# Pre-summed gates written without adding, and table work spread anew over the mixer, in a transformer layer with product-key experts

## The reference, cut to what matters

```
h = layer_norm(alpha * h + mixer(h))                   # z = h @ w_in; attention; s5 scan; glu; up; out
# experts: 8 heads; keys i and j of 128 each
v_half, i_half = top_k(q @ sub_keys, 16)
top_sc, pos = top_k(all sums of one i and one j, 16)
experts = 128 * i + j ;  gates = softmax(top_sc)
act = gelu(einsum('btd,btrkd->btrk', h, u_table[experts]))
y   = einsum('btrk,btrkd->btd', gates * act, v_table[experts])
out = layer_norm(alpha * h + y + ple)
```

## Time and profile before

| | |
|---|---|
| median of 3 runs | 4163.25 us (4162.76 to 4163.94) |
| the profiled execution | 4163.33 us, span in the trace 4161.5 us |
| busy over the span | PE 90%, DVE 67%, POOL 59%, ACT 27% |
| granted clock, mean | 0.958 |
| POOL L829, scatters | 384, 766.4 us busy, mean 1996 ns |
| DVE L1768, turns in the mixer | 162, 192.0 us busy, 370.2 idle ahead of them |
| DVE L2170, dots | 128, 293.1 us busy, 418.6 idle ahead of them |

### The profile page before, as it was taken

How to read it: one execution, slowest core, us unless ns; L and a number is a source line. 1 busy time by engine, 2 the same in 40 slices (tenths; PEclk the granted TensorE clock), 3 DMA queues, 4 the chain that set the end, 5 groups by cost and what they waited for, 6 DMA issues and landing times. The chain is left out here.

```text
span 4161.5 us, 48848 instructions
## 1 busy us (share of the span) xinstructions
PE 3732.4 (90%) x17969; PEld 3234.3 (78%) x17969; DVE 2785.7 (67%) x3191; ACT 1139.3 (27%) x1377; POOL 2446.1 (59%) x1290
## 2 busy tenths in 40 slices
PE   6999999999979999999999558888844999999998
PEld 5777787777767788799999558888843888888887
DVE  7666666667732557695555145555546999999998
ACT  3222222232211422233323112222211323333332
POOL 6333333334434244465555888777786888887871
PEclk9999999999999999999999779999976999999999
DMA  6888888878878578989999468888878999999995
GB/s 226 289 286 291 292 281 288 287 269 293 283 253 272 204 260 325 406 297 337 312 274 277 91 216 295 293 288 278 295 236 298 382 371 396 373 385 383 379 378 194
DMA packets 452613, 1231.10 MB, mean 296 GB/s; under 512 B 120568, under 2 KB 165640, under 8 KB 370984
## 3 DMA queue, kind: packets, MB, share of 16 engines
q1 hardware_dynamic: 261784, 770.07, 53.4%
q0 software_dynamic: 106496, 302.31, 21.2%
q10 hardware_dynamic: 84240, 157.63, 10.3%
HBM read 1020.65 MB, written 344.45 MB: 328 GB/s over the span
## 5 line engine op out<-in xcount | busy, mean ns | idle before, releaser
L764 POOL TENSOR_TENSOR wlo<-raw,whi 128x1024 fp32r<-128x1024 f32 x296 | 755.4, 2574 | 1078.2 <-ACT whi L1117 526.9
L1310 PE MATMUL bank<-h_hi,whi 128*128 128x384 f32 (+1 forms) x3312 | 1206.1, 364 | 191.1 <-DVE wlo L1637 188.0
L1311 PE MATMUL bank<-h_lo,whi 128*128 128x384 f32 (+1 forms) x3312 | 1191.8, 360 | 0.0
L1312 PE MATMUL bank<-h_hi,wlo 128*128 128x384 f32 (+1 forms) x3312 | 1191.8, 360 | 0.0
L829 POOL DMA_INDIRECT gates_d<-sel_g,place_u x384 | 766.4, 1996 | 303.7 <-issue 295.7
L1310 PEld LDWEIGHTS bank<-h_hi,whi 128*128 128x128 f32 x3312 | 633.9, 191 | 257.5 <-DVE wlo L1637 204.5
L1312 PEld LDWEIGHTS bank<-h_hi,wlo 128*128 128x128 f32 x3312 | 633.2, 191 | 50.2
L1311 PEld LDWEIGHTS bank<-h_lo,whi 128*128 128x128 f32 x3312 | 634.0, 191 | 47.7 <-issue 0.2
L1608 PE MATMUL bank<-whi,ew_hi 128*128 128x512 f32 x1408 | 550.3, 391 | 115.1 <-DVE ew_lo L1637 112.3
L1637 DVE TENSOR_TENSOR wlo<-raw,whi 128x2048 fp32r<-128x2048 f32 x240 | 549.0, 2288 | 144.1 <-ACT whi L1236 89.2
L2170 DVE SCALAR_TENSOR_TENSOR u_row<-u_row,h_tok 128x2048 f32<-128x2048 f32 x128 | 293.1, 2290 | 418.6 <-DMA u_row<-u_rows_d,expert_u 418.5
(11 more groups left out here) (299 smaller groups left out, 4645.3 us busy)
## 6 DMA issues: line engine op xcount, KB each, us to landing
raw<-in_weights SPq DMA_DIRECT2D x388, 1024.0 KB
v_rows_d<-in_weights ACTq DMA_DIRECT2D x96, 1024.0 KB
tin<-in_weights SPq DMA_DIRECT2D x162, 512.0 KB, 6.0
u_rows_d<-tout SPq DMA_DIRECT2D x324, 256.0 KB, 6.7
u_rows_d<-u_tout SPq DMA_DIRECT2D x188, 256.0 KB
v_rows_d<-in_weights SPq DMA_DIRECT2D x32, 1024.0 KB
gates_d<-zeros SPq DMA_DIRECT2D x32, 768.0 KB, 17.2
act_d<-act_o ACTq DMA_DIRECT2D x128, 192.0 KB
```

The lines of the kernel that those rows point to most:

```text
L764: pool.tensor_tensor(wlo[slot][:, part], raw[slot][:, part], whi[slot][:, part].bitcast(F32), ALU.subtract).then_inc(lo_made, 1)
L1310: pe.matmul(bank, whi[slot][:, cols], rhs_hi(c), start=c == 0, stop=False)
L1311: pe.matmul(bank, whi[slot][:, cols], rhs_lo(c), start=False, stop=False)
L1312: last = pe.matmul(bank, wlo[slot][:, cols], rhs_hi(c), start=False, stop=c == DC - 1)
```

## The change

1. A scatter no longer adds. From the second head on it writes a gate from `gate_all`, in which DVE's new `sum_gates(k)` has put, for each token and tile, the sum of the gates of the same cell over all picks up to the end of k's head. 112 picks x 3 tiles are 336 scalar_tensor_tensor operations of 128 x 32 to 128 x 128, with a drain ahead of each three, nine in each unit from 16 on, behind the low part. A scatter of tile 0 waits for the sums of its pick.
2. FIRST_SCATTERS 215 instead of 200. Units 16 to 65 turn a slab (50 instead of 47). Dots come 2.25 per unit from unit 69 on, the last in unit 125.
3. OUT has 9 turns instead of 12, three per group. There are two tout buffers; turns of UP and OUT use them alternately, the heads one.
4. In a mixer head slot(3) stands directly behind slot(2), ahead of the wait for h_filled and of the scan; slot(5) ahead of divide(2) and divide(3).
5. Row copies: six per head at b = 0 to 5, 8 in the GLU, 32 in the queries, 16 in the gates stage, 24 in units 0 to 11 (two each).
6. SP in OUT: behind wide load 12 the wait for all stores, ln_g, ln_b, the wait for h_ready, pw_sb, p_sb, then wide loads 13 to 15.

```diff
 HEAD_STEPS = 7 * HEADS - 3
-UP_STEPS, OUT_STEPS = 16, 12
+UP_STEPS, OUT_STEPS = 16, 9
 STEPS = HEAD_STEPS + UP_STEPS + OUT_STEPS
...
 U_ROWS = 3
-U_LAYS = SB - HEADS - N_GLU // 2 - (N_Q // 2 - 1) - N_GATE // 2
-FIRST_SCATTERS = 200
+HEAD_LAYS = 6
+GLU_LAYS_AT = HEAD_LAYS * HEADS // 4
+Q_LAYS_AT = GLU_LAYS_AT + N_GLU // 2
+GATE_LAYS_AT = Q_LAYS_AT + N_Q // 2
+U_LAYS_AT = GATE_LAYS_AT + N_GATE // 4
+U_LAYS = (SB - U_LAYS_AT) // 2
+FIRST_SCATTERS = 215
...
-    return 67 + 4 * k // 7
+    return TURN_U.stop + 3 + 4 * k // 9
...
     tin = [sb(f"tin{h}", [P, HALF], c_at + 4 * h * kb) for h in range(2)]
-    tout = sb("tout", [P, 4, DC, 32], c_at + 8 * kb)
+    tout = [sb(f"tout{k}", [P, 4, DC, 32], c_at + at * kb) for k, at in enumerate((8, 24))]
     u_tout = [sb(f"u_tout{k}", [P, 4, DC, 32], c_at + 8 * k * kb) for k in range(2)]
...
     expert_f = sb("expert_f", [P, PICKS], c_at + 20.5 * kb)
+    gate_all = sb("gate_all", [P, TD, PICKS], c_at + 21 * kb)
+    same = sb("same", [P, TD, PICKS], c_at + 22.5 * kb)
...
     tin_landed = [sm("tin_landed0"), sm("tin_landed1")]
-    tr_made, tout_stored = sm("tr_made"), sm("tout_stored")
+    tr_made = sm("tr_made")
+    tout_stored = [sm("tout_stored0"), sm("tout_stored1")]
     tab_stored = [sm("tab_stored0"), sm("tab_stored1")]
...
         return sum(len(POOL_TILES[n]) for n in range(first))
+    def turned_in(x):
+        q = x - HEAD_STEPS
+        return (0, x) if q < 0 else (1, q // 2) if q % 2 == 0 else (0, HEAD_STEPS + q // 2)
+    TOUTS = [HEAD_STEPS + (STEPS - HEAD_STEPS) // 2, (STEPS - HEAD_STEPS + 1) // 2]
...
                 if x > 0:
-                    store_rows(tout, step_slab(x - 1), tout_stored)
+                    k = turned_in(x - 1)[0]
+                    store_rows(tout[k], step_slab(x - 1), tout_stored[k])
...
                     load_slab(8 * i + b + 2, b % 2)
-                    if b % 2 == 1:
-                        lay_rows(sp, i, b // 2)
+                    if b < HEAD_LAYS:
+                        lay_rows(sp, (HEAD_LAYS * i + b) // 4, (HEAD_LAYS * i + b) % 4)
                     if b == 1:
...
                 table_step(HEAD_STEPS + UP_STEPS - 2 + i)
+            load_wide(AT_OUT, N_OUT - 4)
+            for k in range(2):
+                sp.wait_ge(tout_stored[k], 64 * TOUTS[k] + 64 * (1 - k))
+            sp.dma_start(ln_g[:, :], row(2)).then_inc(ln1_landed, 16)
+            sp.dma_start(ln_b[:, :], row(3)).then_inc(ln1_landed, 16)
             sp.wait_ge(h_ready, TT)
...
             sp.dma_start(p_sb[:, :, :], p_t).then_inc(ple_landed, 16)
-            for i in range(N_OUT - 4, N_OUT):
+            for i in range(N_OUT - 3, N_OUT):
                 load_wide(AT_OUT, i)
-                if HEAD_STEPS + UP_STEPS - 2 + i <= STEPS:
-                    table_step(HEAD_STEPS + UP_STEPS - 2 + i)
-            sp.wait_ge(tout_stored, 64 * (STEPS + 1))
-            sp.dma_start(ln_g[:, :], row(2)).then_inc(ln1_landed, 16)
-            sp.dma_start(ln_b[:, :], row(3)).then_inc(ln1_landed, 16)
             for i in range(2):
...
                     pool.wait_ge(gate_placed[t], 16 * k)
+                if k >= TOPK and t == 0:
+                    pool.wait_ge(gates_summed, TD * (k - TOPK + 1))
                 pool.indirect_dma_start(out=places_d,
                                         out_offset=bass.IndirectOffsetOnAxis(ap=place_u[:, t, k:k + 1], axis=0),
-                                        in_=sel_g[:, t, k:k + 1], in_offset=None, compute_op=ALU.add
+                                        in_=(sel_g if k < TOPK else gate_all)[:, t, k:k + 1], in_offset=None
                                         ).then_inc(gate_placed[t], 16)
...
             pool.wait_ge(tables_made, 1)
-            pool.wait_ge(tout_stored, 64 * (STEPS + 1))
             for k in range(2):
+                pool.wait_ge(tout_stored[k], 64 * TOUTS[k] + 64 * (1 - k))
                 pool.wait_ge(tab_stored[k], 64 * TURNED[k])
...
                     for c in range(2):
-                        lay_rows(act, HEADS + j, 2 * s + c)
+                        lay_rows(act, GLU_LAYS_AT + j, 2 * s + c)
...
-            def queries(start, end, more=None, lays=True):
+            def queries(start, end, more=None):
                 with act.Fori(start, end) as j:
...
                         next_hi(AT_Q, j, s, blk_done, BLK_Q + o)
-                        if lays:
-                            for c in range(2):
-                                lay_rows(act, HEADS + N_GLU // 2 + j, 2 * s + c)
+                        for c in range(2):
+                            lay_rows(act, Q_LAYS_AT + j, 2 * s + c)
                         act.wait_ge(blk_done, BLK_Q + o + 1)
...
             queries(0, DC // 4, squares)
-            queries(DC // 4, DC // 2 - 1)
-            queries(DC // 2 - 1, DC // 2, None, False)
+            queries(DC // 4, DC // 2)
             act.wait_ge(ms_ready, 1)
...
                 next_hi(AT_GATE, o // 2, o % 2, blk_done, BLK_GATE + o)
-                for c in range(2):
-                    lay_rows(act, HEADS + N_GLU // 2 + N_Q // 2 - 1 + o // 2, 2 * (o % 2) + c)
+                lay_rows(act, GATE_LAYS_AT + o // 4, o % 4)
                 if o % 4 == 0 and o > 0:
...
                     if lays:
-                        lay_rows(act, j + SB - U_LAYS, s)
+                        for c in range(2):
+                            lay_rows(act, 2 * j + U_LAYS_AT + s // 2, 2 * (s % 2) + c)
                     act.wait_ge(blk_done, BLK_U + e + 1)
...
-            def turn_slab(x):
-                dve.wait_ge(tout_stored, 64 * x + 64)
+            def turn_slab(x, k=0, used=None):
+                if k == 0:
+                    dve.wait_ge(tout_stored[0], 64 * (x if used is None else used) + 64)
+                elif used > 0:
+                    dve.wait_ge(tout_stored[1], 64 * used)
                 for h in range(2):
                     dve.wait_ge(tin_landed[h], 16 * x + 16)
-                    dve.transpose(out=tout[:, :, 8 * h:8 * h + 8, :].rearrange("p e c i -> p c e i"),
+                    dve.transpose(out=tout[k][:, :, 8 * h:8 * h + 8, :].rearrange("p e c i -> p c e i"),
                                   in_=tin[h][:, :].rearrange("p (c e j) -> p c e j", c=8, e=4)).then_inc(tr_made, 1)
...
                 slot(2)
+                slot(3)
                 dve.drain()
...
                     tt(h_st[:, :, :, 1 + 2**k:], h_st[:, :, :, 1 + 2**k:], ta, ALU.add)
-                    if k == 2:
-                        slot(3)
                     dve.drain()
...
                 bias_and_max(3)
+                slot(5)
                 divide(2)
                 divide(3)
-                slot(5)
                 slot(6)
...
-            with dve.Fori(0, DC // 2) as j:
+            for j in range(DC // 2):
                 for s in range(2):
...
                     split(up_m[:, :].unsqueeze(1), m_hi[:, at, :], m_lo[:, at, :]).then_inc(merged, 1)
-                    turn_slab(HEAD_STEPS + d)
+                    turn_slab(HEAD_STEPS + d, *turned_in(HEAD_STEPS + d))
                     dve.drain()
...
             for g in range(3):
-                for n in range(4):
-                    turn_slab(HEAD_STEPS + UP_STEPS + 4 * g + n)
+                for n in range(3):
+                    x = HEAD_STEPS + UP_STEPS + 3 * g + n
+                    turn_slab(x, *turned_in(x))
                 dve.wait_ge(blk_done, BLK_OUT + 4 * g + 4)
...
+            def sum_gates(k):
+                n = k // TOPK * TOPK + TOPK
+                dve.drain()
+                for t in range(TD):
+                    dve.scalar_tensor_tensor(same[:, t, 0:n], place_f[:, t, 0:n], place_f[:, t, k:k + 1], sel_g[:, t, 0:n],
+                                             ALU.is_equal, ALU.mult, accum_out=gate_all[:, t, k:k + 1]
+                                             ).then_inc(gates_summed, 1)
             dve.wait_ge(h_tok_landed, 64)
-            dots = 0
+            dots, sums = 0, TOPK
             for e in range(U_POOL, N_U):
...
                 low_part_of(e - U_POOL, e % 2, raw[e % 2])
+                while sums < min(PICKS, TOPK + 3 * (e - U_POOL + 1)):
+                    sum_gates(sums)
+                    sums += 1
                 while dots < PICKS and dot_slab(dots) <= e:
...
                     dots += 1
```

More of the change, by code:

```diff
@@ L426, in build_trunk @@
     u_used, acts_made = sm("u_used"), sm("acts_made")
+    gates_summed = sm("gates_summed")
     ew_mul, ew_hi_made = sm("ew_mul"), sm("ew_hi_made")
@@ L719, in _ @@
                                      (g_stored[1], 16), (k_stored, 16), (act_stored[0], 16), (act_stored[1], 16),
-                                     (tout_stored, 64), (out_added, 8),
+                                     (tout_stored[0], 64), (out_added, 8),
                                      (gate_read, 8), (gate_used, 4)):
```

## The result

The changed kernel takes 3983.31 us (median of 4 runs, 3976.05 to 3989.51) against 4163.59 us before; the ratio is 0.957, with a 95% interval of 0.955 to 0.958. The profiled execution took 3989.51 us, span 3987.7. It is faster than forecast by 96 us and lies just under the low end of the range.

The account below looks back on a forecast made before the run. The prediction took POOL's queue of scatters and gathers as the bound from 2343 to 3181, with PE setting the pace in the heads and last stage. 4163.3 - 159 + 103 - 24 - 4 = 4079 us, range 3985 to 4155.

Parts of the forecast that it names:

- the main mechanism: Units to the last stage: scatters that don't add cost POOL's queue 0.94 us at least instead of 1.54, 4.3 per unit.
- the balance of DVE and POOL: Picks before the last stage: 5.0 us each, with DVE at 68% and 2.5 POOL operations of 1.99 us.
- the last stage's figure: Price of a pick: 2.5 operations at the last stage's 2.2 us make 5.5 us; leaning to it gave 5.2.
- its end is 10.1 us later. Nothing hides that: Mixer heads: slot(3) ahead of the scan makes DVE wait, ending the scan 10.1 us later; whole heads term +103 us.
- slot(5)'s 1.3 us: Mixer heads: divide(2) and divide(3) wait behind slot(5), delaying PE's transposes by 0 to 5 us, taken as 1.3.
- The clock's 2 us: Mixer heads: PE's lower granted clock after its longer wait costs at most 5 us each, taken as 2, 16 in all.
- UP and OUT: Stages UP and OUT: two tout buffers let turns skip the store wait, PE sets the pace; -24 us, ends -35 and -10.
- Sums, row copies: Gate sums in units 16 to 53: zero; row copies moved in the gates stage and units: -4 us, ends -10 and +15.
- the first term: Plain scatters, up to the last stage: it starts at 3022 instead of 3181; -159 us, ends -222 and -95.
- C: Scatters stay dear because of their direction, three per unit, 6.1 us per pick; slower, 4258 us; chance 0.16.
- D: Scatters get cheaper, but only three are under way while PE runs; last stage at 3083, 4140 us; chance 0.07.
- B: Mixer heads: unseen slack hides the wait ahead of slot(3), so the heads lose nothing; 3981 us; chance 0.11.

## Why the prediction was right or wrong

**The direction and the main mechanism** were right. The scatter's price went from 1.54 to 0.96 us (I had said 0.94) because it doesn't add, and not more than three adding ones fit in a unit. 4.3 per unit was forecast, 4.5 measured (215 in 394 us). The first dot was forecast at 2352 and came at 2342.7 (with everything up to unit 16 4.5 us late, so 14 us early). Some 10 of these 14 us are the row copies', which I had at nothing there: units 16 to 27 carry none any more, and from unit 16's low part to unit 28's it takes 99.8 us instead of 112.0 (to unit 60's 366.1 instead of 376.3). The plain scatters in the kernel before, with the copies still there, have 111.5; the runs above with the scatters adding again, without sums and with the slots back, without copies there, all have 99.8. I had read unit 67's time off the kernel before. A pick was forecast at 5.2 us and took 5.00, as the balance of DVE and POOL had given; leaning towards the last stage's figure cost 25 us. Against that, the last stage started 26 us after the last dot instead of 10, since PE still had units to do (to 3002). The term was -159, with ends of -222 and -95, and measured -181.

**The step that failed** is in the heads: "its end is 10.1 us later. Nothing hides that". The wait was right to 0.5 us. What I took as fixed was the work behind it: the scan's 26 to 28 us, of which some 12 were DVE waiting for POOL inside its operations (15.3 us busy with the low parts cut), and some 6 of these went; what neg_max then waits for is the work left behind the third low part. They don't show as idle but as long operations, and I had read only the idle times. So neg_max, and PE's wait for it, came 4.7 us later and not 10.1. slot(5)'s 1.3 us were nothing. The clock's 2 us were nearly right: a head grew by 6.0 us, and the 1.3 that are left are the size of what the clock took. In the 6 us behind neg_max, over heads 1 to 7, PE was granted 1.00 in three heads and 0.72 in four before, and 0.50 to 0.73 in all seven now, a mean of 0.59 instead of 0.84, which makes 1.5 us per head (an estimate from these stretches). Together +42 for +103: this is 61 of the 96 us. The lower end of the term, +40, was nearly the value; I had made it for another reason.

**UP and OUT**: right in mechanism, undersized: -36 for -24. With two buffers PE was busy for all of UP, so all of its waiting and the clock's loss came back, and the steps of 12.5 us became 10.9.

**Sums, row copies**: zero, as said; the case in which they are all charged to POOL's queue and the first gather comes 20 us later did not come, as the 215 scatters take as long without the sums. The copies made -1.6 for -4; two per unit cost 4.7 us up to unit 16, which the gates stage's 6.3 outweigh, and what they gave back behind unit 16 is in the first term. The prediction also says that 12 of 28 copies leave the units; it is 4, as 24 stay.

**Rivals.** C, slower, fell with 0.96 us; the run with adding scatters shows that its arithmetic was right once a scatter does cost 1.54: last stage at 3206 with the heads' delay in it, the time 206 us above the changed kernel's. (The gain that is left at 5.9 us per pick is 70 us by the prediction's own terms, not the 85 it gives.) D fell: four or five were issued per unit. B, with nothing lost in the heads, gave 3981, which is nearly the time measured, by a wrong path: the heads did lose 42 us, and 22 and 12 us that I had not counted came from elsewhere. A total that agrees doesn't show that its terms do.

The range's low end lies 2 us above the measured time. Its 94 us don't follow from the ends as they are given: one large term at its fast end makes 63, both make 126, which would have been 3953. All three large terms moved the same way, by 22, 61 and 12 us.

## What to carry to other kernels

An operation that takes several times as long as its like beside it is a wait that the idle times don't show: before moving work past it, ask with what it collides and whether it still will. Look for which other engine's operation runs at that time, and subtract the collisions that the move avoids from its price, or add those that it brings. And let one operation per cell write what another engine has summed ahead, if that other engine has room: the one edit was the whole gain here. The rearrangements around it cancelled, 36 us won in UP and OUT against 42 lost in the heads, and only runs of single pieces showed which of them to keep.

## What the runs showed of the hardware

The exclusion of DVE and POOL works in both directions. I had used it in one, POOL's scatter held until a dot's end. In the other, a DVE operation with two SBUF inputs is held for the rest of POOL's two-input operation: a 128x240 pair of 0.73 us took 4.97 beside a low part, and 0.73 in the same place when the low part was cut to 64 columns; a STREAM_TRANSPOSE pair, with one input, took 2.37 us beside it as without. The Trainium skill says as much ("SBUF — State Buffer", section "SBUF: two separate sides": whichever of the two starts first gets the port pair for the whole instruction, "the other fully blocks"); the trace agrees, with some 6 us per head.

An indirect scatter that adds costs GpSimd 1.54 us to issue and a plain one 0.96, with the same 128 elements; and with the weights' loads going on, three adding ones were issued per unit of 8.28 us and four to five plain ones. What limits their number in flight no run here shows.

A row copy of 1 MB from HBM to HBM beside a unit that loads a slab and turns it costs that unit 0.9 to 1.0 us: 12 units with one copy each took 112.0 us and without 99.8, and 8 of them 73.4 and 66.6. Six copies per mixer head cost no more than four.
